# Opening by halves, dilated log counts as matmuls, and the second scale section multiplied in the second norm

## What is computed

```python
mod = silu(c) @ w_mod[l] + b_mod[l]
sh1, sc1, gt1, sh2, sc2, gt2 = split(mod, 6)
h = rms_norm(x, g_norm_mix[l]) * (1 + sc1) + sh1
q_d, k_d, v_d, cq, ckv, k_rope = split(h @ w_in[l], cuts)      # 512, 512, 512, 256, 128, 32 columns
o_dil = dilated_attention(norm(q_d), norm(k_d), v_d, positions, slopes)   # 8 heads of 64
o_mla = latent_attention(cq, ckv, k_rope, positions, ...)      # 8 heads, rotated part of 32
x = x + gt1 * (concat([o_dil, o_mla]) @ w_out[l])
h = rms_norm(x, g_norm_mlp[l]) * (1 + sc2) + sh2
x = x + gt2 * (square(relu(h @ w_mlp_in[l])) @ w_mlp_out[l])
```

## Time and profile before

| what | value |
|---|---|
| time, median of 3 runs | 1695.75 us (1695.21 to 1695.86) |
| profiled execution: its own time | 1694.58 us |
| its span, first to last instruction | 1692.8 us |
| TensorE busy | 1656.1 us, 98% |
| VectorE busy | 1198.4 us, 71% |
| ScalarE busy | 963.5 us, 57% |
| GpSimd busy | 88.6 us, 5% |
| granted TensorE clock, mean | 0.999 |
| read from memory | 379.12 MB, 225 GB/s over the span |

### The profile page before, as it was taken

One profiled execution on the slowest core, in us unless ns is written; L12 is line 12 of the kernel. 1 busy time (PEld: TensorE's weight loads), 2 busy tenths in 40 slices (PEclk: granted clock), 3 DMA queues, 4 the chain that ended last, 5 costly groups with the idle time before them and its releaser, 6 DMA issues.

```text
span 1692.8 us, 26664 instructions
## 1 busy us (share of the span) xinstructions
PE 1656.1 (98%) x10402; PEld 1422.0 (84%) x10402; DVE 1198.4 (71%) x1491; ACT 963.5 (57%) x1274; POOL 88.6 (5%) x105
## 2 busy tenths in 40 slices
PE   7999999999999999999999999999999999999998
PEld 5767898887688998898999999899888787887876
DVE  3775887777678555657585545557589888999887
ACT  4675534456754444546564434546567777667765
POOL 2050000003300000000000000000000000000000
PEclk9999999999999999999999999999999999999999
DMA  9765788845368655643256555553356999999995
GB/s 342 279 208 173 271 278 283 278 138 176 119 235 288 198 186 187 196 150 125 100 177 212 185 184 187 178 172 101 121 191 225 351 331 332 345 320 344 341 336 179
DMA packets 266362, 381.64 MB, mean 225 GB/s; under 512 B 8299, under 2 KB 201121, under 8 KB 266258
## 3 DMA queue, kind: packets, MB, share of 16 engines
q1 hardware_dynamic: 264592, 377.26, 66.8%
q0 software_dynamic: 1104, 1.76, 0.3%
q10 hardware_dynamic: 562, 1.18, 0.2%
HBM read 379.12 MB, written 1.05 MB: 225 GB/s over the span
## 4 chain that ended last, share of the span: by engine, by line
PE 83%; DVE 8%; ACT 4%; POOL 2%; issue 2%; DMA 1%; ACTq 0%; DVEq 0%
PE bank L2194 71%; DVE w_low L1270 4%; PE bank L2253 3%; ACT w_high L665 3%; PE bank L2509 1%; PE bank L2751 1%; DMA raw<-in_w_mod_dram 1%; PE bank L2539 1%; DVE mod_sums L1388 1%; PE bank L2301 1%; DMA x<-in_x_dram 1%; DVE turned L1351 1%; POOL dilated_bias L628 1%; POOL dilated_bias L629 1%; PE bank L2744 1%
## 5 line engine op out<-in xcount | busy, mean ns | idle before, releaser
L1270 DVE TENSOR_TENSOR w_low<-raw,w_high 128x2048 fp32r<-128x2048 f32 (+2 forms) x315 | 690.0, 2194 | 226.5 <-ACT w_high L665 225.0
L665 ACT ACTIVATE w_high<-raw 128x2048 fp32r<-128x2048 f32 (+3 forms) x333 | 596.4, 1797 | 219.3 <-PE bank L2194 211.0
L2194 PE MATMUL bank<-h_high,w_high 128*128 128x256 f32 x1200 | 342.8, 286 | 0.2
L2194 PE MATMUL bank<-h_high,w_low 128*128 128x256 f32 x1200 | 339.8, 283 | 0.0
L2194 PE MATMUL bank<-h_low,w_high 128*128 128x256 f32 x1200 | 339.8, 283 | 0.0
L2194 PE MATMUL bank<-w_high,h_high 128*128 128x512 f32 (+2 forms) x768 | 301.0, 392 | 8.5 <-DVE w_low L1270 7.5
L2194 PE MATMUL bank<-w_high,h_low 128*128 128x512 f32 (+2 forms) x768 | 292.1, 380 | 0.0
L2194 PE MATMUL bank<-w_low,h_high 128*128 128x512 f32 (+2 forms) x768 | 291.7, 380 | 0.0
L2194 PEld LDWEIGHTS bank<-h_high,w_high 128*128 128x128 f32 x1200 | 230.1, 192 | 5.3 <-issue 3.4
L2194 PEld LDWEIGHTS bank<-h_low,w_high 128*128 128x128 f32 x1200 | 230.1, 192 | 1.2
L2194 PEld LDWEIGHTS bank<-h_high,w_low 128*128 128x128 f32 x1200 | 230.0, 192 | 0.0
(11 more groups left out here) (355 smaller groups left out, 1822.4 us busy)
## 6 DMA issues: line engine op xcount, KB each, us to landing
raw<-in_w_gu_exp_dram SPq DMA_DIRECT2D x160, 512.0 KB, 5.4
raw<-in_w_in_dram SPq DMA_DIRECT2D x52, 1024.0 KB, 5.3
raw<-in_w_mod_dram SPq DMA_DIRECT2D x48, 1024.0 KB, 5.9
raw<-in_w_dn_exp_dram SPq DMA_DIRECT2D x40, 1024.0 KB, 6.4
raw<-in_w_mlp_in_dram SPq DMA_DIRECT2D x32, 1024.0 KB, 5.9
raw<-in_w_mlp_out_dram SPq DMA_DIRECT2D x32, 1024.0 KB, 5.2
raw<-in_w_gu_dense_dram SPq DMA_DIRECT2D x22, 1024.0 KB, 5.1
raw<-in_w_out_dram SPq DMA_DIRECT2D x16, 1024.0 KB, 5.1
```

The source lines that it names most:

```text
L665: return nc.scalar.activation(dst, src, ACT.Copy, scale=scale)
L1270: V.tensor_tensor(wlo[w % SPLIT][:, 0:n], raw[raw_of(w) % RAW][:, 0:n], whi[w % SPLIT][:, 0:n].bitcast(F32), ALU.subtract).then_inc(raw_us ...
L2194: ins = T.matmul(out, lhsT, rhs, start=start and i == 0, stop=stop and i == len(pairs) - 1)
```

## The change

*Opening by halves.* The first two sections come in quarters of 512 columns by 512 rows: two quarters each give four blocks of h. The load order becomes: four quarters, w_in's first half of K for the latent columns (piece 0) and for the dilated queries (now piece 1), three quarters, the second half for the latent columns (now piece 2), the last quarter, the second half for the queries (piece 3). TensorE accumulates the strips in a bank; `store_first(half)` transposes them. `store_rows`, `c32` and the columns form are gone.

*Third section.* (0, 2) goes by rows; its store on VectorE stands ahead of piece 6's low part.

*Log counts.* TensorE adds the log counts to the scores, as high and low part times an identity: four passes a head. GpSimd makes only the product for the bias, and the rotation of the latent queries.

*Second scale section.* (l, 4) is loaded behind piece 13, and multiplied between the turns of x in the second norm; its store stands in the norm, and half of piece 15's low part, which stood there, goes ahead of the last two additions to x.

```diff
-    after = {(0, 0): [-1, -1, 0, 1], (0, 1): [-1, -1, 0, 1], (0, 2): [2, 3, 4, 5]}
+    after = {(0, 0): [-1, -1, 1, 1], (0, 1): [-1, -1, 1, 2], (0, 2): [3, 4, 5, 5]}
-        after[l, 4] = [l * L1 + W_HEADS] * 4
+        after[l, 4] = [l * L1 + W_IN_LAST + N_OUT] * 4
-                           key=lambda v: (v[0], max(v[1], 1), v[2], v[1]))
+                           key=lambda v: (v[0], v[1], v[2]))
-BY_ROWS = ((0, 3), (0, 4), (1, 3), (1, 4))
+BY_ROWS = ((0, 2), (0, 3), (0, 4), (1, 3), (1, 4))
...
+        def rotate_queries(l):
+            n = ROPE // 2
+            heads = qup.rearrange("p t (h d) -> p t h d", d=DH + ROPE)
+            x1, x2 = heads[:, :, :, DH:DH + n], heads[:, :, :, DH + n:DH + ROPE]
+            pool.wait_ge(rows_normed, 2 * l + 1)
+            for i, (part, v) in enumerate(zip(q_parts, (x1, x2, x2, x1))):
+                ins = nc.gpsimd.tensor_tensor(part, v, q_trig[:, i, :, :].unsqueeze(2).to_broadcast([P, TT, H, n]), ALU.mult)
+            step(ins)
+            nc.gpsimd.tensor_tensor(x1, q_parts[0], q_parts[1], ALU.subtract)
+            nc.gpsimd.tensor_tensor(x2, q_parts[2], q_parts[3], ALU.add).then_inc(mla_norm, 1)
...
             for h in range(H):
                 if h == 2:
                     spread_key()
+                elif h == 4:
+                    rotate_queries(l)
...
-                step(nc.gpsimd.tensor_scalar(dst[:, :], dist[:, :], -(2.0 ** -(h + 1)), None, ALU.mult))
-                nc.gpsimd.tensor_tensor(dst[:, :], dst[:, :], con[:, C_LNM:C_LNM + TT * S], ALU.add).then_inc(bias_ready, 1)
+                nc.gpsimd.tensor_scalar(dst[:, :], dist[:, :], -(2.0 ** -(h + 1)), None, ALU.mult).then_inc(bias_ready, 1)
...
             norm_squares(0)
             store_rs(0)
+            high(range(2))
             split_to(0)
+            high(range(2, 4))
+            split_to(2)
+            high(range(4, KD))
...
-            split_to(w + 2)
-            split_to(w + 3)
-            act.wait_ge(used, w + 2)
+            split_to(w + 4)
+            act.wait_ge(used, w + 3)
             store_product(4, 1536, W_IN - 1536)
...
+        def store_first(half):
+            dve.wait_ge(mod_product, 4 * half + 4)
+            c = slice(4 * half, 4 * half + 4)
+            step(V.transpose(mod_turned, first_strips(half)))
+            step(V.tensor_tensor(modc[:, 0:2, c], columns, biases[:, :, c], ALU.add))
+            step(V.scalar_tensor_tensor(modc[:, 1, c], modc[:, 1, c], 1.0, vec[...], ALU.add, ALU.mult))
+            V.sem_inc(mod_stored, 1)
+        def first_norm():
+            for half in range(2):
+                store_first(half)
+                for k in range(4 * half, 4 * half + 4):
                     scaled_block(0, k, scale_of)
+                    if k % 4:
+                        low_part(0, k - 1, shift_of)
+                low_part(0, 4 * half + 3, shift_of)
+                if half == 0:
+                    rest_to(2)
...
             rest_to(w + 2)
             if l == 0:
                 store_vectors()
-            rest_to(w + 3)
+            rest_to(w + 4)
...
             V.tensor_tensor(latlo, latent, lathi.bitcast(F32), ALU.subtract).then_inc(lat_low, 1)
+            if l == 0:
+                store_mod(0, 2)
             rest_to(w + 6)
...
-            store_mod(l, 4)
...
                 add_to_x(6 + t, t, 0, 0).then_inc(x_mixed, 1)
+            rest_part(w + N_OUT + 1, 0)
             dve.wait_ge(out_first, l + 1)
             add_to_x(0, 0, 1, 0).then_inc(x_mixed, 1)
             dve.wait_ge(used, w + 4)
             add_to_x(1, 1, 1, 0).then_inc(x_mixed, 1)
...
-            norm(2 * l + 1, ..., None, lambda: rest_part(w + 1, 0))
+            norm(2 * l + 1, ..., None, lambda: store_mod(l, 4))
...
             for i in range(begin, 4):
                 turn_quarter(n, i)
+                if n % 2 and i:
+                    multiply_mod(n // 2, 4, i - 1)
+                elif n and i in (1, 2):
                     keep_busy(2, idle_bank, w)
+            if n % 2:
+                multiply_mod(n // 2, 4, 3)
+                keep_busy(1, 1, w)
+                spread_rs(n)
+                keep_busy(7, 1, w)
...
+        multiply_first(0, 1)
         spread_rs(0)
         turn_idly(2)
+        multiply_first(1, 0)
+        turn_idly(2)
+        multiply_first(1, 1)
+        turn_idly(2)
+        keep_busy(4, 5, 0)
...
+        natural(0, 0, W0, [psum[4 + t] for t in range(TT)], True, False, 0)
+        multiply_first(0, 2)
+        natural(1, 0, 512, [psum[6 + t] for t in range(TT)], True, False, None, [0])
+        multiply_first(0, 3)
+        natural(1, 0, 512, [psum[6 + t] for t in range(TT)], True, False, None, [1])
+        multiply_first(1, 2)
+        turn_idly(4, 1)
+        multiply_first(1, 3)
+        turn_idly(4, 1)
+        later_chunk(4, W0, 2)
         pe.wait_ge(loaded, 16 * N_LOADS)
         T.transpose(psum[0][:, 0:N_ROWS], stage, ident).then_inc(setup_t, 1)
...
+            natural(w + 3, 4, 512, [psum[6 + t] for t in range(TT)], False, True)
+            if l == 0:
+                turn_positions()
+                multiply_mod(0, 2, 0)
+            pe.wait_ge(proj_out, 4 * l + 1)
+            natural(w + 4, 0, 512, [psum[4 + t] for t in range(TT)], True, False)
+            if l == 0:
+                pe.wait_ge(setup_v, SETUP_TRIG - 1)
+                multiply_mod(0, 2, 1)
             pe.wait_ge(lat_norm, l + 1)
...
+            natural(w + 5, 4, 512, [psum[4 + t] for t in range(TT)], False, True)
             if l == 0:
                 multiply_mod(0, 2, 2)
                 multiply_mod(0, 2, 3)
+            pe.wait_ge(lat_low, l + 1)
             w += 6
+            if l == 0:
+                pe.wait_ge(mod_stored, stored_of(0, 2))
...
+                pe.wait_ge(counts_ready, l + 1)
+                for e in range(2):
+                    for t in range(TT):
+                        for i, counts in enumerate((counts_high, counts_low)):
+                            ins = T.matmul(psum[e][:, S * t:S * t + S], ident_high, counts[:, S * t:S * t + S],
+                                           start=False, stop=i == 1, skip_group_check=True)
+                    ins.then_inc(head_scored, 1)
...
-                if gp == 4:
-                    pe.wait_ge(mod_stored, stored_of(l, 3))
-                multiply_mod(l, 4, gp - 4)
                 spread_sums(gp)
...
-            multiply_mod(l, 4, 3)
```

More of the change, by code:

```diff
@@ L96, in mod_units @@
 def mod_units():
-    units = [(0, n % 2, n // 2, (n % 4,)) for n in range(8)]
-    for l, s in SECTIONS[2:]:
-        if (l, s) in BY_ROWS:
-            continue
-        if (l, s) in BY_PRODUCT:
-            units += [(l, s, q, (q,)) for q in range(4)]
-        else:
+    units = []
+    for l, s in SECTIONS:
+        if (l, s) not in BY_PRODUCT:
             units += [(l, s, 2 * i, (2 * i, 2 * i + 1)) for i in range(2)]
@@ L475, in _ @@
             w = l * L1
-            load_natural(a["w_in"][l], w, [(1536, W_IN - 1536), (0, 512), (512, 512)])
+            for half in range(2):
+                for i, (c0, n) in enumerate(((1536, W_IN - 1536), (0, 512))):
+                    load(raw_of(w + 2 * half + i), rows_of_k(a["w_in"][l])[:, 4 * half:4 * half + 4, c0:c0 + n])
+                    load_behind(w + 2 * half + i)
+            load_natural(a["w_in"][l], w + 4, [(512, 512)])
             w += 6
@@ L1532, in _ @@
             V.sem_inc(lat_norm, 1)
-            rest_to(w + 4)
             if l == 0:
@@ L1588, in _ @@
             k_rows = k_nat.rearrange("p t (h d) -> p t h d", d=DH + ROPE)
-            q_parts = [rtmp[:, i, :].rearrange("p (t h d) -> p t h d", t=TT, d=half) for i in range(2)] + \
-                [nat[:, :, 1536 + P * i:1664 + P * i].rearrange("p t (h d) -> p t h d", d=half) for i in range(2)]
             def head_rs(c, n):
@@ L1659, in _ @@
             max_head(0, 1)
-            if l == 0:
-                store_mod(0, 2)
-            else:
+            if l:
                 refine(48)
@@ L1707, in _ @@
             dve.wait_ge(x_mixed, 4 * l + 4)
-            norm(2 * l + 1, lambda k: modc[:, 3, k:k + 1], lambda k: modc[:, 2, k:k + 1], None, lambda: rest_part(w + 1, 0))
+            norm(2 * l + 1, lambda k: modc[:, 3, k:k + 1], lambda k: modc[:, 2, k:k + 1], None, lambda: store_mod(l, 4))
             rest_part(w + 1, 1)
@@ L2369, in _, with turn_idly @@
         pe.wait_ge(setup_a, 1)
-        multiply_first(0)
-        reduce_first(0)
+        multiply_first(0, 0)
         turn_x(0, 0)
         T.transpose(psum[5][:, 0:112], first_rows, ident[0:112, 0:112]).then_inc(setup_t, 1)
-        multiply_first(1)
-        reduce_first(1)
+        def turn_idly(count, bank=5):
+            for _ in range(count):
+                T.matmul(psum[bank][:, S:2 * S], ident, x[:, 0, 0:S], start=True, stop=True)
+        multiply_first(0, 1)
         spread_rs(0)
-        def turn_idly(count):
-            for _ in range(count):
```

(20 more changed lines are left out.)

223 lines of the change are left out of this document (63 added, 160 removed).

## The result

The changed kernel takes 1713.15 us (median of 4 runs, 1711.39 to 1714.04), the kernel before beside it 1695.65: a ratio of 1.0102, 95% interval 1.0085 to 1.012. It is slower by 17.5 us, where 9.2 were forecast (the range ended at 1711). The profiled execution took 1714.04 us for a span of 1712.1, and its last matmul starts 18.05 us behind that of before.

The account below looks back on a forecast made before the run. TensorE, busy 98% of the span, was taken as the bound. Opening 5.0, third section 2.5, dilated rounds -0.2 and -0.3, latent rounds -7.4 and second norm 9.6 summed to +9.2, giving 1705.0 us; the range took in 1697.4 and ended at 1711.

Parts of the forecast that it names:

- clock falls: Rival: TensorE's stands of about 3 us in opening and second norm drop it to 1.2 GHz; 1709 to 1712, chance 0.06.
- Opening: +5.0 forecast: From start to the positions: VectorE's later low parts delay w_in and piece 3; +5.0 us, bounds +1 to +7.5.
- that the diff doesn't speak of: Opening: VectorE's low part of piece 3 stands behind store_vectors, so TensorE waits 3.2 us ahead of piece 3.
- The rival that transfers set the opening: Opening: last quarter products end with the last transfer, near 39.5 us, gaining 2.6; 1697.4, chance 0.10.
- Third section: +2.5 forecast: Layer 0, ahead of piece 6: store_mod(0, 2) and then the low part follow the last product; +2.5 us, bounds +2.2 to +4.3.
- Dilated rounds: -0.2 and -0.3 forecast: Layers 0 and 1: the wait for GpSimd vanishes but TensorE's added passes fill its place; bounds -3 and +4 for both.
- my 1.0 a pair: Dilated rounds: TensorE's eight added passes cost 1.0 us per pair with the switch, 4.0 a layer.
- The rival of 18 us: Dilated rounds follow GpSimd alone, so dropping its additions in two layers gives 18 us; 1687.5, chance 0.06.
- rotation late: Rival: VectorE's operations stretch GpSimd's query rotation from 4.0 to 6 us or more, 2 us a layer; 1709, chance 0.04.
- Latent rounds: -3.7 a layer forecast: Four products a layer leave TensorE's path in the latent rounds; -3.7 a layer, -7.4 in all, bounds -8 and -5.
- Second norm: +4.8 a layer forecast: Second norm: late piece 15 delays squares and last additions, and products follow the last turn; +4.8 a layer, +9.6 in all.
- +1.0 for a piece in time: Second norm's lower bound and rival: piece 15 lands by 163, costing +1.0 a layer; 1697.4, chance 0.08.

Follow-up runs that it names:

- fill: Changed kernel with extra idle matmuls where TensorE stands still (ahead of w_in, piece 3, piece 6, in both second norms): ratio 1.0058 to the kernel before.
- order3: Changed kernel with VectorE's low part of piece 3 put ahead of store_vectors: ratio 1.0067 to the kernel before.
- low6: Changed kernel with VectorE's low part of piece 6 put ahead of store_mod(0, 2): ratio 1.0074 to the kernel before.
- counts_on_before: Kernel before with only the log counts part: TensorE adds them, GpSimd rotates the latent queries: ratio 1.0002.
- move_on_before: Kernel before with only (l, 4) multiplied in the second norm, one quarter loaded behind piece 13 and three behind piece 15: ratio 0.9985.
- split14: Changed kernel with the first quarter of (l, 4) loaded behind piece 13 and the other three behind piece 15: ratio 1.0045 to the kernel before.
- behind15: Changed kernel with all four quarters of (l, 4) loaded behind piece 15 in place of piece 13: ratio 1.0113 to the kernel before.
- undo4: Changed kernel with the part about (l, 4) undone: loaded behind the heads' pieces, multiplied in the latent rounds again: ratio 1.0058 to the kernel before.
- both_on_before: Kernel before with the log counts part and (l, 4) multiplied in the second norm, one quarter loaded behind piece 13, three behind piece 15: ratio 0.9981.

## Why the prediction was wrong in size

The direction, the places and the waits were right, and the clock was missing from the sum; the likeliest case summed to 1705.0 and the range ended at 1711. Term by term, in distances of the traces:

**The clock: the step that failed.** The prediction took "clock falls" as a rival with a chance of 0.06 beside its sum, because today's gaps under 1.5 us have no fall, and gave it 1709 to 1712, of which the range took in only 1711. It should have been a term: the forecast itself put stands of about 3 us at three places of TensorE's path (before w_in, before piece 3, before the last additions) and one of 2.5 before piece 6. The runs showed six falls and 9 us for them (fill), which is the whole of 18.05 - 9.2; five of them came with those stands, the sixth at 1289 us without one. I had no row of a fall behind a gap of 3 us. From 15 us on the longest gap in the trace of before is 1.45, so a gap of 3 was outside what its rows could vouch for, and its price could have been bounded from the earlier trace rows: passes that take 4.5 us take 9.0 at the lower level.

**Opening: +5.0 forecast.** w_in began at 29.82 and not at 28.8: half of that is x, which landed 0.5 later in that execution. The passes of piece 0 took 6.27 for 4.67 and those of piece 3 7.36 for 5.78, both in part at 0.50. Without these 3.2 the product of (0, 2, 0) stands 6.3 behind in place of 9.5: the term itself was 1.3 short, within its bounds. The wait "that the diff doesn't speak of" was 2.90 for 3.2 (order3). The rival that transfers set the opening is refuted: the last quarter landed at 36.3 and was multiplied at 46.84.

**Third section: +2.5 forecast.** The gap is 2.77 and a further 1.5 is the half clock in piece 6; low6 shows both.

**Dilated rounds: -0.2 and -0.3 forecast.** Layer 0 gave -1.3 (from 13.9, less the latent 3.7 to 8.9), layer 1 -0.7 in its first projection and +0.15 in the rounds. counts_on_before sets the part at +0.2 and +0.15: my 1.0 a pair was about right (a batch of eight passes took 1.15 in the trace after), and so was that the wait for GpSimd, once gone, is filled by TensorE. The rival of 18 us is refuted. In "rotation late" only the size came: the six operations took 5.2 us and not 4.0.

```profile
112.37 1.45 POOL L607 TENSOR_TENSOR rope_products<-turned 128x256 f32<-128x256 f32 x2
113.77 1.42 POOL L607 TENSOR_TENSOR natural<-turned 128x256 f32<-128x256 f32 x2
115.28 1.59 POOL L609 TENSOR_TENSOR turned<-rope_products 128x256 f32<-128x256 f32 x1
116.83 0.73 POOL L610 TENSOR_TENSOR turned<-natural 128x256 f32<-128x256 f32 x1
```

The same form takes 1.59 once (the subtraction) and 0.73 once (the addition). The Trainium skill (GPSIMD Engine Reference, Specifications) says that VectorE's two-input work contends with GpSimd's; the pair agrees with that: VectorE had an operation with both inputs in SBUF at work for 1.0 us of the 1.59 (1.24 from 115.04 on) and none beside the 0.73. No run here separates it. TensorE did not wait for the bias behind it; VectorE did once, for 0.77 us at 120.87.

**Latent rounds: -3.7 a layer forecast.** 3.6 and 3.7 in the changed kernel, 3.7 and 3.7 in move_on_before, where nothing else changed: right.

**Second norm: +4.8 a layer forecast.** 6.4 and 6.1 in the changed kernel, 4.8 and 4.8 in fill, where no fall lies in it; so the term was exact and the half clock is the rest. Its parts hold as well: piece 15 landed in 5.72 for 5.9, and split14 takes 4.3 of the cost in layer 0 away, which is 2.7 for the wait (4.8 less 2.1) and 1.6 for the fall that goes with it. What I put at +1.0 for a piece in time measured 2.1: the chain of split14 goes from the fourth product through store_mod (0.9 us) to the first block, and I had hidden store_mod beside spread and copy.

**Sum.** Without falls, 9.1 in the traces against 9.2. That this is so near is in part luck: ahead of the rounds fill without its batches stands at 9.2, where 7.5 was forecast, and the rounds gave back 1.3 and about 0.5, where 0.2 and 0.3 were. One fall more lay where I did not look at all, at 1289 us, 770 us behind the last edited line.

## What to carry to other kernels

A wait on TensorE's path is priced as its own length plus what the work behind it loses at half the clock: here stands of 2.4 to 3.05 us brought 1.3 to 1.7 more each, and matmuls that compute nothing took that back. Not each stand pays it: of 24 stands of over 2.4 us in the six traces that have them (after, order3, low6, behind15, split14, undo4) 18 had a fall in them or within 2 us behind them. The kernels without a stand over 1.5 us had one fall between them in the first 1260 us, in the opening of both_on_before. Whoever forecasts a gap longer than any in the trace should add the clock to the sum and not to the rivals.

When weights stream through a fixed ring of buffers, moving a product later holds its buffers later: ask for every piece behind it whose buffer it inherits, and not only for the first (behind15 mended piece 15 and lost at piece 17). Here one quarter before and three behind piece 15 was worth 10 us over four in a row, the falls that went with the wait included.

Where a low part that TensorE needs next and a wait for TensorE share VectorE's queue, the low part belongs first: order3 and low6 gave back 6 and 5 us, in part by falls of the clock that did not come.

## What was not expected of the hardware

The granted clock in one unchanged opening differs between executions: 1.00 from 15.0 us in the trace of before, 0.50 from 20.9 to 31.1 us in that of both_on_before, with TensorE busy for 2.19 of the 3.3 us ahead. With the later rise ahead of it, that moves w_in by 4.3 us. On the chip of that run the kernel before lay between 1695.9 and 1700.9, with a mean granted clock from 0.999 down to 0.995.

A fall came at about 1270 to 1290 us in the changed kernel, order3, low6, split14 and move_on_before and not in the other nine traces, though the gaps there are alike (0.39 and 0.84 us in move_on_before, 0.39 and 0.83 in before). What decides it stays open. The Trainium skill (TensorE: Matmul & The Clock Gate, Part 1) says that the low level is the default and that activity releases it; the traces agree in that each fall but those at a trace's very end ended while TensorE worked, and none shows why equal work was once granted 1.00 and once 0.50.
